# The second attention's value shift in pieces of 112, 15 and 1 rows, and the low pieces of a late weight tile two steps behind its high pieces

## The reference, cut to what matters

```python
def _stick_breaking(q, k, v):
        mask = kpos[None, :] < qpos[:, None]
        z = jnp.einsum('bhqd,bshd->bhqs', qb, k).astype(jnp.float32) * scale
        log_beta = jax.nn.log_sigmoid(z)
        log_1mb = jnp.where(mask, jax.nn.log_sigmoid(-z), 0.0)
        suffix = lax.cumsum(log_1mb, axis=3, reverse=True) - log_1mb
        a = jnp.where(mask, jnp.exp(log_beta + suffix), 0.0)
        return jnp.einsum('bhqs,bshe->bhqe', a.astype(v.dtype), v)

def _sb_layer(x, k, v, norm_g, w_in, w_out):
    proj = _rms(x, norm_g) @ w_in
    q, g = jnp.split(proj, [SB_W], axis=-1)
    o = _stick_breaking(q.reshape(b, s, SB_HEADS, SB_HEAD_DIM), k, v)
    o = o.reshape(b, s, SB_W) * jax.nn.silu(g)
    return x + o @ w_out
```

## Time and profile before

| What | us |
|---|---|
| Median of the runs | 2457.83 |
| The profiled execution's own time | 2457.59 |
| Its span in the trace | 2455.8 |
| TensorE busy | 2281.5 (93%) |
| VectorE busy | 1512.5 (62%) |
| ScalarE busy | 952.0 (39%) |

### The profile page before, as it was taken

One profiled execution on the slowest core, in us unless ns is written; L12 is line 12 of the kernel. 1 busy time (PEld: TensorE's weight loads), 2 busy tenths in 40 slices (PEclk: granted clock), 3 DMA queues, 4 the chain that ended last, 5 costly groups with the idle time before them and its releaser, 6 DMA issues.

```text
span 2455.8 us, 29670 instructions
## 1 busy us (share of the span) xinstructions
PE 2281.5 (93%) x12574; PEld 1159.9 (47%) x12574; DVE 1512.5 (62%) x1959; ACT 952.0 (39%) x1396; POOL 203.4 (8%) x246
## 2 busy tenths in 40 slices
PE   7999999999999999999999789999997339998999
PEld 5445444444444444445444566544443114655655
DVE  6898857776667757787422799755342021765762
ACT  5245335322222323433323887423230011665750
POOL 0001030000000003533101000120000000000000
PEclk9999999999999999999999999999998669999999
DMA  5110001111110111121210100211301000001021
GB/s 182 35 69 35 1 35 38 65 61 43 69 69 35 37 68 68 37 104 52 81 40 1 35 1 1 104 35 69 137 30 59 26 25 34 1 1 35 1 86 52
DMA packets 51732, 120.16 MB, mean 49 GB/s; under 512 B 2650, under 2 KB 8339, under 8 KB 51216
## 3 DMA queue, kind: packets, MB, share of 16 engines
q1 hardware_dynamic: 48616, 105.40, 12.1%
q10 hardware_dynamic: 2984, 12.87, 1.3%
HBM read 101.49 MB, written 12.58 MB: 46 GB/s over the span
## 4 chain that ended last, share of the span: by engine, by line
PE 77%; DVE 10%; DMA 8%; ACT 4%; issue 1%; ACTq 0%; SPq 0%; DVEq 0%
PE PS L72 72%; DMA OV<-R 6%; PE PS L75 5%; ACT RG L81 2%; DVE R L93 2%; DVE RG L101 1%; DVE R L101 1%; DVE RG L104 1%; DMA RG<-in_a_w_in 1%; ACT R L81 1%; DVE scl L110 1%; DVE oss L110 1%; DVE RG L107 1%; DVE dg L104 1%; DVE mx L110 0%
## 5 line engine op out<-in xcount | busy, mean ns | idle before, releaser
L72 PE MATMUL PS<-R,RG 128*128 128x512 f16 (+1 forms) x5568 | 1205.5, 378 | 103.0 <-DVE R L101 98.5
L72 PEld LDWEIGHTS PS<-R,RG 128*128 128x128 f16 (+1 forms) x5568 | 554.2, 104 | 747.0 <-DVE R L101 86.7
L72 PE MATMUL PS<-RG,R 128*128 128x512 f16 (+2 forms) x3080 | 604.6, 363 | 3.0 <-DVE R L93 2.5
L72 PEld LDWEIGHTS PS<-RG,R 128*128 128x128 f16 (+1 forms) x3080 | 281.0, 106 | 301.4 <-issue 18.5
L101 DVE SCALAR_TENSOR_TENSOR RG<-RG,scl 128x4096 f16<-128x4096 f32 (+2 forms) x70 | 213.2, 3053 | 101.3 <-ACT RG L81 101.3
L81 ACT ACTIVATE RG<-RG,scl 128x4096 f16<-128x4096 f32 (+2 forms) x70 | 177.8, 2556 | 232.3 <-DVE scl L113 232.3
L107 DVE TENSOR_TENSOR_SCAN RG<-RG,dg 128x128 f32<-128x128 f32 (+7 forms) x128 | 167.0, 1346 | 100.2 <-ACT RG L81 99.9
L101 DVE SCALAR_TENSOR_TENSOR R<-PS,scl,R 128x512 f32<-128x512 f32 (+1 forms) x211 | 148.6, 743 | 115.8 <-PE PS L72 109.2
L110 DVE TENSOR_REDUCE scl<-RG 128x1 f32<-128x4096 f32 (+1 forms) x35 | 150.3, 4293 | 99.7 <-DMA RG<-in_w_ff 41.4
L122 POOL PARTITION_ALL_REDUCE scl<-scl x49 | 34.6, 709 | 1727.9 <-DVE scl L110 1447.9
L75 PE MATMUL PS<-ident,RG 128*128 128x128 f32 x864 | 148.7, 287 | 25.6 <-DVE RG L107 15.5
(11 more groups left out here) (141 smaller groups left out, 1675.0 us busy)
## 6 DMA issues: line engine op xcount, KB each, us to landing
RG<-in_w_ff SPq DMA_DIRECT2D x16, 2048.0 KB, 8.5
RG<-in_a_w_in SPq DMA_DIRECT2D x8, 2048.0 KB, 8.9
xspill<-R ACTq DMA_DIRECT2D x2, 4096.0 KB, 15.3
RG<-in_w_kv SPq DMA_DIRECT2D x4, 2048.0 KB, 8.0
RG<-in_b_w_in SPq DMA_DIRECT2D x4, 2048.0 KB, 7.9
RG<-in_w_in SPq DMA_DIRECT2D x3, 2048.0 KB, 8.4
R<-in_x SPq DMA_DIRECT2D x8, 512.0 KB, 7.9
RG<-in_w_out SPq DMA_DIRECT2D x2, 2048.0 KB, 7.8
```

What stands on the lines that cost most here:

```text
L72: return self.engine.matmul(*a, **k) if self.engine else Nothing()
```

## The change

There are two edits. In the value shift, the copy of 127 rows becomes two copies, of the last 15 rows and of the first 112; the copy of one row stays, and so do the bytes, the buffers, the waits and the total that the semaphore must reach before the subtraction (each copy adds 16). In the attention, low piece y of tile 40 is written at step y + 2 in place of step y; the high pieces stay where they are. The last low piece, which signals `weight(40)`, is then at step 37 in place of 35.

```diff
@@ vector
-                if z in sb_pieces:
-                    s = w_slot(40)
-                    e.wait_ge(*sig("w_high").at(40, z))
-                    low_half(piece(s, z), piece(s[:, 4096:8192], z), piece(w_raw(40), z), w_col(40, 2)).then_inc(
-                        *(sig("weight").up(40) if z == sb_pieces[-1] else step.up()))
+                if z - 2 in sb_pieces:
+                    s, y = w_slot(40), z - 2
+                    e.wait_ge(*sig("w_high").at(40, y))
+                    low_half(piece(s, y), piece(s[:, 4096:8192], y), piece(w_raw(40), y), w_col(40, 2)).then_inc(
+                        *(sig("weight").up(40) if y == sb_pieces[-1] else step.up()))
@@ scalar
-                        e.dma_start(before[1:128, :], V2[0:127, t, :]).then_inc(*done.up(t, by=16))
+                        e.dma_start(before[113:128, :], V2[112:127, t, :]).then_inc(*done.up(t, 1, by=16))
+                        e.dma_start(before[1:113, :], V2[0:112, t, :]).then_inc(*done.up(t, by=16))
```

## The result

The changed kernel takes 2322.43 us, the median of four runs (2320.87 to 2324.76), beside 2457.72 us for the kernel before (four runs). The ratio is 0.9451, with a 95% interval of 0.9435 to 0.9467: 5.5% faster. The forecast was 2325.

What follows compares the result with a forecast made beforehand. TensorE bounds the kernel, except where it waits on copies run by one DMA engine and, in the attention, on scans held behind low pieces. 2457.59 - 112.7 - 19.8 = 2325.1 us; own range 2320 to 2331, 8 in 10 2320 to 2338.

Steps and rivals of the forecast that it cites:

- Start, 112.7 us for the copies: Query and gate products: seven products at full pitch save 111.3 us, the next 12 at full clock another 1.4.
- part 1: Value shift: splitting each tile's 127-row copy into 15 and 112 rows removes TensorE's waits, 112.7 us in sum.
- Landing time 4 us, spare to about 9: Value-shift copies: each lands in 4 us (bounds 2.0 and 19.9); TensorE does not wait unless landing passes about 9.
- may double L for one round: Value shift: the 2 MB weight load shares the engines some 8 us and may double the copies' landing time once.
- Issues, 1.9 us a step: ScalarE's queue: issuing three copies takes some 1.9 us a step, against 5.18 us for a product.
- Spread over 16 and 15 engines: Value-shift copies: 112 rows spread over 16 DMA engines, 7 rows each, and 15 rows over 15, one each.
- Part 2, 19.8 us: Attention steps 28 to 35: low pieces two steps later cut 61.3 to 41.0 us; 20.3 less 0.5 gives 19.8.
- The 0.5 us that I took off for step 33: Attention: ScalarE in step 33 has a sum of 1.05 us on top and is over its time; 0.5 us deducted.
- Slow pieces: Rival, value shift: three copies add up and share engines with the load, landing 12 to 15 us; 2340 us, chance 0.07.
- a moved wait: Rival, attention: ScalarE or VectorE holds the scans and half of the 19.8 us stays; 2335 us, chance 0.08.
- no spread: Rival, value shift: both pieces stay on one engine, so the copies' split gains nothing; 2438 us, chance 0.03.
- the slower case: Rival, value shift: pieces stay on one engine, each extra transfer costs its fixed part; 2470 at 4 us, chance 0.01.

## Why the prediction was right, point by point

**Start, 112.7 us for the copies.** By the trace, TensorE's first transposes of step 28 came 114.94 us earlier (2192.23 to 2077.29). 1.98 of that lies ahead of the change (the tile 38 measure starts that much earlier), so 112.96 is part 1. The two terms behind it, 111.3 for the seven products at full pitch and 1.4 for the clock of the next twelve, hold: seven products take 36.08 us (147.59 before) and the next twelve, 1911.52:1973.70, 62.18 us (63.61 before), and TensorE has no wait for L101.

**Landing time 4 us, spare to about 9.** The larger pieces in 1840:1910 of the kernel after, with KB each and median us from issue to landing:

```profile
OV<-R ACTq DMA_DIRECT2D x8, 448.0 KB, 3.8
```

The estimate of 4 us was good, though its rows were of stores of other shapes, so that part of it was luck. The waits after t = 7 and t = 6 are 5.44, 1.73 and 0.51 us, and only three of eight subtractions wait at all. The load "may double L for one round": from the end of its issues (1859.90) the copy for t = 5 took 6.8 us, the one for t = 3 3.1 us. The low half of step 10 is begun at 1895.08, and product 18 wanted it at 1911.5 (1913.5, less the 1.98 us): 16 us to spare, the lower end of the 16 to 20 that were worked out. Where a cost begins was put at 9 us of landing. The kernel with 124 and 3 rows tests that: its three rounds have 13.9, 9.2 and 9.3 us of landing, 10.8 in the mean, and TensorE waits 3.0 us. The 9 us held 4.4 us back for the measure of tile 39; here that measure (1894.14) fell inside the last landing and cost nothing, and without it the same working gives 10.8 us. Since the first subtraction of that kernel also waited 1.92 us, a wait of about 2 us was due. So the place was worked out soundly and on the careful side.

**Issues, 1.9 us a step.** Three issues take 2.00 to 2.30 us, so the one-row and 127-row issues of the earlier trace rows were about the right price. ScalarE's bank copies behind the issues came late twice: VectorE waited 0.97 us each for them (before its low halves at 1860.57 and 1870.63), which cost TensorE nothing.

**Spread over 16 and 15 engines.** This was the step on which all of part 1 hung, and I had no row for it, only the rule of the Trainium skill's page "DMA: Bandwidth & Descriptors" ("Why a DMA increments its semaphore by 16 and not by 1"). The row counts bear it out for this kernel: 113 rows give a period of 17.89 us, 122 rows 9.74 us and a share of 0.13, 124 rows a share of 0.25, and 112 rows a share of 0.80 in a burst; with 126 and 112 rows TensorE waits for nothing there. That it is just 16, 15 or 14 engines for 112, 15 or 126 rows no row counts out.

**Part 2, 19.8 us.** Steps 28 to 35 took 40.81 us against 41.0 forecast, so the gain is 20.49. The 0.5 us that I took off for step 33 was not lost; the pitch of 5.31 us against my 5.32 is the same, and TensorE has no wait in 2077:2130.

**Sum.** 112.96 + 20.49 = 133.45 us by the trace, against 132.5 forecast. The rest of the difference of 135.4 between the spans is the 1.98 us ahead of the change. The forecast of 2325 is above 2322.4 for these two reasons, a gain 0.95 us larger and the 1.98 us, and the second is scatter: in ten traces of kernels that are alike up to there, that instruction starts anywhere in 5.6 us.

**The rivals.** Slow pieces, a moved wait, no spread and the slower case did not come. Both pieces on one engine would not quite have been "gives nothing": with 113 and 14 rows the small piece takes its rows off the crowded engine, and 14 us were won. The rule against splitting a copy by partitions (the Trainium skill's page "DMA: Bandwidth & Descriptors", "Rules for kernel authors") would have had the landing times add up; instead the median of the pieces of 112 rows is 3.8 us. The page gives its advice for the two halves of a 128-partition transfer, and no run here has one. For 127 rows one transfer was the slowest of the six ways that ran, and the measurement decides.

## What to carry to other kernels

When a copy sets the pace, divide its bytes by its period: 26 GB/s with a DMA share of 1/16 means one engine, and then it is the number of rows in the copy, here from 127 or 113 to 112, 124 or 126, not the number of bytes or of copies, that has to change. An operand that is produced by another engine at the end of a step is best consumed a step later if nobody needs the result, since a wait in an in-order queue holds everything behind it: here it held the scans, for 20 us in eight steps. And work out how much longer than expected a transfer may take before it reaches the bottleneck: with eight banks of distance the copies had several us each to spare, and neither the load beside them nor 126 rows in place of 112 mattered, while 124 rows, at 9 us and more of landing, began to.

## What the runs showed of the hardware that I had not expected

The instruction that issues a DMA can itself become slow. On ScalarE's queue an issue of the copies took 0.52 to 1.18 us in the changed kernel, up to 8.65 us in the one before and up to 6.21 us with 113 and 14 rows; the load of the mask behind them took 0.35, 4.35 and 2.32 us to issue. Copies still in flight alone don't do this: with 122 and 5 rows every subtraction waits for its copy too, and no issue took more than 0.84 us. In the slow cases over a hundred rows of a copy lay on one engine; where the limit is, no run shows.

Also, the 2 MB weight load needed 20.9 us to land beside the slow copies and 8.8 in the changed kernel. My reading, which no run tests by itself, is that its shares on the other engines were done early and the load was complete only when the share on the crowded one was. The trace before fits it: the load is issued at 1858.14, its queue has moved 2.01 of the load's 2.10 MB by 1868, and the DMA share falls from nine tenths to that of one engine at about 1866, but the load lands only at 1879.
